# Key page scores of the first attention phase moved behind the decay sums, and the value sets of the decode step placed anew

## The reference, cut to what matters

```python
logits = jnp.einsum('nqhd,nkhd->nhqk', q, k) * (FA_HEAD_DIM ** -0.5)
decay = c_q[..., :, None] - c_k[..., None, :]          # c = cumsum(log forget values)
p = jax.nn.softmax(where(causal, logits + decay, -inf))
o = jnp.einsum('nhqk,nkhd->nqhd', p, v)
y = (o * jax.nn.silu(z)) @ w_out + b_out
x = layer_norm(alpha * x + (1 + gate) * y)
```

## Time and profile before

| | |
|---|---|
| median of 3 runs | 1765.38 us (1764.94 to 1765.78) |
| the profiled execution | 1757.93 us, span 1756.3 us, mean granted TensorE clock 0.975 |
| PE / PEld busy | 1643.2 us (94%) / 1428.1 us (81%) |
| DVE busy | 1011.8 us (58%) |
| ACT / POOL busy | 623.8 us (36%) / 420.2 us (24%) |
| DMA | 197.90 MB, mean 113 GB/s |

### The profile page before, as it was taken

The page is one execution under the profiler, slowest core; times in us unless marked ns, Lnnn a source line. Parts: engine busy times, 40 slices in busy tenths (PEclk is TensorE's granted clock), DMA queues, the critical chain, the costliest instruction groups (busy, mean ns, idle before and its releaser), DMA issues.

```text
span 1756.3 us, 27853 instructions
## 1 busy us (share of the span) xinstructions
PE 1643.2 (94%) x10080; PEld 1428.1 (81%) x10080; DVE 1011.8 (58%) x1571; ACT 623.8 (36%) x980; POOL 420.2 (24%) x414
## 2 busy tenths in 40 slices
PE   6999989999999998999887999999999999979965
PEld 4899989999999997999865777787777777757742
DVE  3433353433433437225566888879797977689436
ACT  2222122112112117224442646463636455463221
POOL 0240010110111100001221626262534344250020
PEclk8999999999999998999998999999999999999987
DMA  8481112222222221324324242424333221243474
GB/s 363 158 315 36 48 61 93 77 72 95 72 72 96 73 71 56 109 92 154 118 72 135 84 113 69 120 74 118 97 95 97 84 72 72 73 133 132 159 283 194
DMA packets 85777, 197.90 MB, mean 113 GB/s; under 512 B 16898, under 2 KB 47234, under 8 KB 83922
## 3 DMA queue, kind: packets, MB, share of 16 engines
q1 hardware_dynamic: 73154, 141.97, 24.9%
q0 software_dynamic: 12560, 55.10, 8.9%
HBM read 171.31 MB, written 34.39 MB: 117 GB/s over the span
## 4 chain that ended last, share of the span: by engine, by line
PE 77%; DVE 9%; issue 5%; DMA 3%; ACT 3%; POOL 2%; POOLq 0%; SPq 0%; DVEq 0%; ACTq 0%
PE bank L1826 20%; PE bank L1827 19%; PE bank L1828 19%; PE bank L2188 2%; PE bank L2142 2%; PE bank L2190 2%; PE bank L2189 2%; PE bank L1961 2%; PE bank L2170 1%; DVE bank L1479 1%; PE bank L2169 1%; POOL p_lo L640 1%; DMA pages<-cache_v 1%; PE bank L1941 1%; PE bank L2045 1%
## 5 line engine op out<-in xcount | busy, mean ns | idle before, releaser
L1826 PE MATMUL bank<-h_hi,w_lo 128*128 128x344 f32 x1152 | 374.5, 325 | 9.9 <-DVE h_lo L1125 8.7
L1827 PE MATMUL bank<-h_lo,w_hi 128*128 128x344 f32 x1152 | 369.0, 320 | 0.0
L1828 PE MATMUL bank<-h_hi,w_hi 128*128 128x344 f32 x1152 | 368.7, 320 | 0.0
L640 POOL TENSOR_TENSOR p_lo<-parg,p_hi 128x512 fp32r<-128x512 f32 (+1 forms) x192 | 226.8, 1199 | 161.4 <-ACT p_hi L966 160.7
L1826 PEld LDWEIGHTS bank<-h_hi,w_lo 128*128 128x128 f32 x1152 | 217.7, 189 | 14.8 <-issue 12.2
L1826 PE MATMUL bank<-x_hi,w_lo 128*128 128x512 f32 x528 | 222.1, 421 | 6.6 <-POOL x_lo L592 6.5
L1827 PEld LDWEIGHTS bank<-h_lo,w_hi 128*128 128x128 f32 x1152 | 217.8, 189 | 0.2 <-issue 0.2
L1828 PEld LDWEIGHTS bank<-h_hi,w_hi 128*128 128x128 f32 x1152 | 217.7, 189 | 0.0
L1827 PE MATMUL bank<-x_lo,w_hi 128*128 128x512 f32 x528 | 209.7, 397 | 0.0
L1828 PE MATMUL bank<-x_hi,w_hi 128*128 128x512 f32 x528 | 209.6, 397 | 0.0
L1826 PE MATMUL bank<-y_hi,w_lo 128*128 128x320 f32 (+2 forms) x512 | 177.4, 346 | 13.7 <-DVE w_lo L1083 6.5
(11 more groups left out here) (300 smaller groups left out, 2622.5 us busy)
## 6 DMA issues: line engine op xcount, KB each, us to landing
raw<-units SPq DMA_DIRECT2D x121, 512.0 KB, 3.5
scr_k<-cache_k POOLq DMA_DIRECT2D x32, 512.0 KB, 5.4
ada_ring<-w_ada SPq DMA_DIRECT2D x32, 512.0 KB, 3.3
pages<-cache_v POOLq DMA_DIRECT2D x32, 512.0 KB, 6.1
kpb<-scr_k SPq DMA_DIRECT2D x24, 512.0 KB, 4.1
ada_first<-w_ada SPq DMA_DIRECT2D x8, 1024.0 KB, 14.8
KX<-KA SPq DMA_DIRECT2D x32, 256.0 KB, 6.9
ckb<-scr_c POOLq DMA_DIRECT2D x16, 512.0 KB, 4.7
```

The lines of the kernel that those rows point to most:

```text
L640: g.tensor_tensor(p_lo[:, r, off:HALF], parg[:, r, off:HALF], p_hi[:, r, off:HALF].bitcast(F32), ALU.subtract).then_inc(S("p_ready"), 1)
L1826: mm(out, lhs_lo, rhs_hi, start=first, stop=False)
L1827: mm(out, lhs_hi, rhs_lo, start=False, stop=False)
L1828: return mm(out, lhs_hi, rhs_hi, start=False, stop=last)
```

## The change

**First phase.** On SP, the q row and the first key group of phase 0 are taken from ahead of `load_phase(0)` and issued inside it, after `KX` and raw unit (1,0), and after a wait for both rows of `ckb`. On VectorE, phase 0's four `score_mul` and `score_sum` pairs each stand one place later; the fourth is behind `kq_low(1, 0)` at the phase's end. The other phases are as before.

**Value sets.** Sets 4 and 5 go to slots 0 and 1, after sets 2 and 3; sets 6 and 7 go to slots 2 and 3, after the projection. On TensorE sets 0 and 1 are used at halves 9 and 10 (before: 11 and 12), sets 2 and 3 at halves 13 and 14 (before: between the first transposes of the end), sets 4 and 5 between the first transposes, 6 and 7 after those of block 3.

**The end.** On SP the eight `fsw` transfers also wait until all pages of sets 6 and 7 are in. `mask_o`, `gated_s` and the `fs_row` copies stand one block earlier on VectorE, `d_o`, the `fsw` matmuls, the fold and the sample's sums two blocks (the sums one) earlier on TensorE. `pages_in2` now counts sets 6 and 7.

```diff
--- before.py
+++ after.py
@@ -272,10 +272,10 @@
 
         LATE = KB - 2
         MOVED = 16 * 2 * NS * NP
-        VALUE_SLOT = (0, 1, 0, 1, 2, 3, 0, 1)
+        VALUE_SLOT = (0, 1, 0, 1, 0, 1, 2, 3)
         VALUE_IN = {0: ("pages_in0", MOVED + 16 * NP), 1: ("pages_in1", 16 * NP), 2: ("pages_in0", MOVED + 32 * NP),
-                    3: ("pages_in1", 32 * NP), 4: ("pages_in2", 32 * NP), 5: ("pages_in2", 32 * NP),
-                    6: ("pages_in0", MOVED + 48 * NP), 7: ("pages_in1", 48 * NP)}
+                    3: ("pages_in1", 32 * NP), 4: ("pages_in0", MOVED + 48 * NP), 5: ("pages_in1", 48 * NP),
+                    6: ("pages_in2", 32 * NP), 7: ("pages_in2", 32 * NP)}
         SCORED = 4 * KB
 
         KIND = (0, 1, 2, 3)
@@ -456,6 +456,12 @@
             def load_phase(j, scored):
                 load_swapped(j)
                 load_b(j + 1, 0)
+                if isinstance(j, int) and j == 0:
+                    for h in range(2):
+                        sp.wait_ge(S(f"ckb_in{h}"), 16)
+                    load_query(0)
+                    sp.wait_ge(S("pages_in0"), MOVED)
+                    load_keys(0, 0)
                 load_b(j + 1, 1)
                 load_keys(j, 1)
                 load_b(j + 1, 2)
@@ -473,9 +479,6 @@
             for q in range(4):
                 load_b(0, q)
             sp.wait_ge(S("ln1_back"), TT)
-            load_query(0)
-            sp.wait_ge(S("pages_in0"), MOVED)
-            load_keys(0, 0)
             load_phase(0, True)
             with sp.Fori(1, LATE - 1) as j:
                 load_phase(j, True)
@@ -520,6 +523,7 @@
 
             sp.wait_ge(S("r2_ready"), 2 * KB)
             sp.wait_ge(S("lo_ready"), U_FS)
+            sp.wait_ge(S("pages_in2"), 32 * NP)
             for b in range(KB):
                 sp.dma_start(fsw[:, b, :, :], units[U_FA - WB + b, :, :, :]).then_inc(S("fsw_in"), 16)
 
@@ -696,12 +700,10 @@
             for n in range(NS):
                 if n < 2:
                     pool.wait_ge(S("pages_used"), SCORED - 4 + 4 * n)
-                elif n < 4:
+                elif n < 6:
                     pool.wait_ge(S("pages_used"), SCORED + n - 1)
-                elif n == 4:
+                elif n == 6:
                     pool.wait_ge(S("fa_mm"), 2 * KB)
-                elif n >= 6:
-                    pool.wait_ge(S("pages_used"), SCORED + n - 3)
                 load_values(n)
             for name, n in (("vn_out", 16), ("k_out", 16 * KB), ("v_out", 16 * KB), ("kqv_s_out", 16)):
                 pool.wait_ge(S(name), n)
@@ -1582,6 +1584,8 @@
 
             def phase(j, more, keys):
                 later = not isinstance(j, int) or j > 0
+                late_keys = keys and not later
+                keys = keys and later
                 take_samples(j, 2)
                 kq_low(j, 1)
                 evac_s(j, 2)
@@ -1615,6 +1619,8 @@
                 z_gate(j, 0)
                 exponents(j, 2)
                 z_evac(j, 1)
+                if late_keys:
+                    score_mul(j, 0)
                 if keys:
                     score_mul(j, 1)
                 exponents(j, 3)
@@ -1623,6 +1629,8 @@
                 z_gate(j, 1)
                 if later:
                     invert(j - 1, 1, 1)
+                if late_keys:
+                    score_sum(j, 0)
                 if keys:
                     score_sum(j, 1)
                 if more:
@@ -1633,6 +1641,8 @@
                 gate_o(j, 0)
                 exponents(j, 5)
                 invert(j, 0, 0)
+                if late_keys:
+                    score_mul(j, 1)
                 if keys:
                     score_mul(j, 2)
                 exponents(j, 6)
@@ -1641,6 +1651,8 @@
                 invert(j, 0, 1)
                 exponents(j, 7)
                 divide_o(j, 0)
+                if late_keys:
+                    score_sum(j, 1)
                 if keys:
                     score_sum(j, 2)
                 if more:
@@ -1650,9 +1662,13 @@
                     evac_s(j + 1, 1)
                     split_lo(j + 1, 2)
                 exponents(j, 9)
+                if late_keys:
+                    score_mul(j, 2)
                 if keys:
                     score_mul(j, 3)
                 exponents(j, 10)
+                if late_keys:
+                    score_sum(j, 2)
                 if keys:
                     score_sum(j, 3)
                 if not more:
@@ -1661,6 +1677,9 @@
                 exponents(j, 11)
                 if more:
                     kq_low(j + 1, 0)
+                    if late_keys:
+                        score_mul(j, 3)
+                        score_sum(j, 3)
                 else:
                     lo(U_FA + 1, (U_FA + 1) % 2)
                     for k in range(2, KB - 1):
@@ -1791,29 +1810,32 @@
 
             layer_norm_stats(0, TT)
             layer_norm_stats(1, TT)
-            for t in range(2, 5):
-                finish(t - 2)
-                layer_norm_stats(t, TT)
+            finish(0)
+            layer_norm_stats(2, TT)
+            finish(1)
+            layer_norm_stats(3, TT)
+            finish(2)
+            mask_o()
+            layer_norm_stats(4, TT)
             finish(3)
-            mask_o()
+            gated_s()
             layer_norm_stats(5, TT)
             finish(4)
-            gated_s()
-            layer_norm_stats(6, TT)
-            finish(5)
             for h in range(2):
                 dve.wait_ge(S("fs_used"), h + 1)
                 v.tensor_copy(fs_row[:, h * 512:(h + 1) * 512], bank(6 + h)).then_inc(S("fs_row"), 1)
-            layer_norm_stats(7, TT)
-            finish(6)
+            layer_norm_stats(6, TT)
+            finish(5)
             dve.wait_ge(S("fs_used"), 3)
             link(v.tensor_tensor(rS[:, :, :], bank(5)[:, 0:KB * NS].rearrange("p (a b) -> p a b", b=NS),
                                  wide(col("fa_b_out"), NS), ALU.add))
             residual_s(x1S[:, :, 0:NS])
             norm_sum(rS[:, :, :], KB)
-            finish(7)
+            layer_norm_stats(7, TT)
+            finish(6)
             norm_square(3, rS[:, :, :], KB, rS[:, :, :])
             norm_var(3)
+            finish(7)
             norm_out(3, KB, "ln_g", KB, "ln_b", rS[:, :, :]).then_inc(S("ys_ready"), 1)
 
 
@@ -2366,24 +2388,28 @@
                         decode_logits()
                     if n == 8:
                         decode_weights()
-                    if n == 11:
+                    if n == 9:
                         decode_values(0)
-                    if n == 12:
+                    if n == 10:
                         decode_values(1)
+                    if n == 13:
+                        decode_values(2)
+                    if n == 14:
+                        decode_values(3)
 
             pe.wait_ge(S("r2_ready"), 2 * KB)
             ln_forward(0, r2T, TT)
             ln_forward(1, r2T, TT)
-            for n in range(2, 6):
+            for n in range(4, 6):
                 decode_values(n)
-                ln_forward(n, r2T, TT)
+                ln_forward(n - 2, r2T, TT)
             decode_values(6)
             decode_values(7)
             pe.wait_ge(S("d_step"), 4)
             for c in range(KB):
                 last = mm(bank(4)[:, c * NS:(c + 1) * NS], omask[:, c * P:(c + 1) * P], maskp[:, :], start=True, stop=True)
             last.then_inc(S("d_o"), 1)
-            ln_forward(6, r2T, TT)
+            ln_forward(4, r2T, TT)
             pe.wait_ge(S("d_step"), 5)
             pe.wait_ge(S("fsw_in"), 16 * KB)
             for h in range(2):
@@ -2391,13 +2417,15 @@
                     rows = slice(32 * (k % 4), 32 * (k % 4) + NS)
                     last = mm(bank(6 + h)[rows, :], oS[:, k, :], fsw[:, 4 * h:4 * h + 4, k, :], start=k < 4, stop=k >= 4)
                 last.then_inc(S("fs_used"), 1)
-            ln_forward(7, r2T, TT)
+            ln_forward(5, r2T, TT)
             for h in range(2):
                 pe.wait_ge(S("fs_row"), h + 1)
                 for b in range(4 * h, 4 * h + 4):
                     last = mm(bank(5)[:, b * NS:(b + 1) * NS], fs_row[:, b * P:(b + 1) * P], fold4[:, 0:NS], start=True, stop=True)
             last.then_inc(S("fs_used"), 1)
+            ln_forward(6, r2T, TT)
             sample_sum(3, 0)
+            ln_forward(7, r2T, TT)
             sample_sum(3, 1)
```

## The result

The changed kernel takes 1773.66 us (median of 6 runs, 1770.83 to 1777.14), the kernel before 1765.12 beside it (6 runs, 1758.99 to 1765.78). The ratio is 1.0064, 95% interval 1.005 to 1.0077: slower, by less than 1%. (The two medians are 8.5 us apart; the ratio, by which the runs are compared from here on, stands for 11.3 us.) The profiled execution of after has a span of 1772.3 us and took 1773.79; that of before had 1756.3. The difference of these two, 16.0 us, is more than the runs show, since the profiled execution of before is among its shortest. Whole spans don't serve for a few us: the issue of `scr_c`, ahead of which TensorE does the same work in all kernels here, falls at 922.9 us in one trace and at 928.4 in another.

What follows compares the result with a forecast made beforehand. It took TensorE to bound the kernel nearly everywhere, broken by waits for the decay sums' transfers and the last value page. -7 + 0.5 + 12.9 = +6.4 us on 1765.4 gave 1771.8 us, range 1763.5 to 1778.

Steps and rivals of the forecast that it cites:

- -6.5: First phase: net forecast in us, from -7 for the decay rows and +0.5 for the late keys.
- Decay rows, "issued by POOL at the same moment": First phase: POOL's issues stay at 931.6 and 932.1, rows land earlier, TensorE's stall falls to 3.8 us; -7 us.
- the first phase gives back everything: Rival, first phase: stall and half clock both vanish, 12.7 us, if decay rows land in 3.8 us; 1766.1; 12 in 100.
- Late keys, +0.5 (0 to 4): End of first phase: SP's row comes about 8 us later, key page (1,0) and raw (2,0) having little slack; +0.5 us.
- covered, with 1.1 us to spare: First phase's end: the fourth score pair, 2.4 us, fits VectorE's 3.5 us wait; key page 3 lands in time.
- End, +12.9: Kernel's end: pages land earlier, but `fsw` waits for them, y_out(0) for `fsw`, mask_o for y_out(0); +12.9 us.
- If the clock stays up: Final chain after y_out(0): the end's loss would be about 3 us less.
- y_out served at once: Rival, end: `fsw` does not hold up y_out(0), landing 2.6 us after issue; not slower, 1764.7; 14 in 100.
- First part does nothing: Rival, first phase: `KX` and k_out fill the engines alone, no gain there; +13.4 us, 1778.8; 12 in 100.

Runs made afterwards that it cites:

- e1: The change's first-phase edit alone (SP and VectorE) on the kernel before, value sets and end as before: 1752.84 us, ratio 0.9951.
- e2: All edits of the change but those of the first phase, against the kernel before: 1782.61 us, ratio 1.0121.
- e5: e1 with the 4 KB q-row write back ahead of the phase, its broadcast and the key page still late: 1760.29 us, ratio 0.9988.
- e3: The kernel before with only VectorE's later score products and sums in phase 0, SP's queue as before: 1763.82 us, ratio 1.0018.
- e6: e1 with raw block (1,3) issued ahead of the last key group in phase 0: 1756.27 us, ratio 0.9961 to the kernel before.
- e9: e7 with SP waiting in phase 0 for keys and raw blocks to land before the small q-row write: 1746.23 us, ratio 0.9901 to before.
- e7: Changed kernel with three y blocks ahead of `fsw` and before's end order on VectorE and TensorE, value sets still moved: 1740.48 us, ratio 0.9878 to before.
- e11: First-phase edit and three y blocks ahead of `fsw`, with value sets and end order as in the kernel before: 1748.93 us, ratio 0.9922 to before.
- e8: e7 and e6 together, raw block (1,3) ahead of the last key group in e7: 1746.04 us, ratio 0.9907 to the kernel before.
- e4: Changed kernel with y_out(0) and y_out(1) ahead of `fsw` and its page wait on SP: 1761.94 us, ratio 0.9994 to the kernel before.

## Why the prediction was right, and where its steps were not

The sign and the shape held: a gain in the first phase, a larger loss at the end, because the weights now wait for the pages, the y block for the weights, and the mask for the y block. 1771.8 was forecast, 1773.66 measured. The closeness is in part luck. The terms sum to +6.4, where the two medians give +8.5 and the ratio +11.3; the base of 1765.4 was the median of three runs, 3 us above the 1762.1 of the many runs beside the experiments, and made up for a part of it. And the two halves were wrong in opposite directions: the first phase gained more than -6.5 (-8.6 by e1), the end lost more than +12.9 (+21.3 by e2).

*Decay rows, "issued by POOL at the same moment".* This step failed. The issue hung on the landing of `scr_c`, and that on the small q-row write, which the edit takes away: 3.4 us earlier (e5 tells this from the 1.05 MB). With it the stall went, to 0.6 us and not to 3.8, and the granted clock stayed at 1.00. By the mark the gain was 11.6 us where 7 was forecast; the rival "the first phase gives back everything" (12.7) was near the truth in size, though not by the landing of 3.8 us that it asked: the rows took a median of 5.9.

The Trainium skill (DMA: Bandwidth & Descriptors, Queues, rings and completion order) says that a transfer's completion signal lands only after all earlier writes of the same DMA engine, whatever their queue. The traces agree for `scr_c`, issued behind the small write: 6.1 to 6.3 us in the four kernels that have the write there (before, e2, e3, e5), 2.2 in those that don't. The rule doesn't give the other half: raw (1,3) and, in e6, the key group are issued ahead of the write and are late too.

*Late keys, +0.5 (0 to 4).* The border gave back 2.6 us, inside the range, but "covered, with 1.1 us to spare" failed. VectorE had the time for the fourth pair, but POOL was at `p_lo` beside it and TensorE needed that: 1.0 us, in e3 and e9 as in after. The rest was SP's queue: in before SP comes to the small write 4.3 us after raw (1,3) (1003.71 and 1007.99), in after 0.6 us. So it was raw (1,3), and not the key pages or raw (2,0) that the text watched; raw (2,0) held up e1 and e9 a little later in the phase. That the write's nearness does it rests on e6 and e9; neither was faster.

*End, +12.9.* The mechanism held at each point, the size was off: +23.6 us in the traces (of it 1.3 ahead of the projection's half n = 4, in some traces with either end and not in others), +21.3 by e2. On the scale of the projection's last `fg`: pages in at 17.0 (forecast 14.9; the last lands 7.8 us after issue, not 5.3); y_out(0) issued at 20.8 (19.4) and landed at 33.1 (29.1), 12.3 us after issue and not 9.7; from there to the end 52.6 us (47.8). In the last piece the mask's and the fold's matmuls take 3.58 us each at half clock, where the sum had those of before at full clock (1.95 and 1.85 us), and VectorE waits up to 7.0 us for block 5's transposes, forecast 6. Together these make the time from the last `fg` to the span's end 8.9 us longer than forecast. "If the clock stays up" was given as a chance of 3 us less; the trace went the other way.

*y_out served at once* fell: 12.3 us. *First part does nothing* fell with e1.

What stays open: why a write of 4 KB takes 8.4 to 13.8 us here, and by what path it holds a transfer issued before it. No run changed its layout.

## What to carry to other kernels

Before a buffer-bound step is put ahead of a chain that ends the kernel, ask what its buffer waits for: here taking two calls (`mask_o` and `gated_s`) out from behind `finish(2)` was worth 14 us, and taking the first two stores out from behind the weights 12. Each is measured with the other left as it was; they act on the same wait, so they don't simply add. In this kernel, value work moved into a busy stage paid only where the transfers at its end were issued in the order in which they were needed: the same sets lost 21 us with the stores and the mask in the wrong place (e2), and gained 8 with both put right (e7 against e11). Work moved into another engine's idle time is not free when a third engine works beside it: look at what runs there. And when an issue time is carried over as unchanged, follow its releaser back one more step.

## Hardware behaviour that was not expected

A 4 KB write that the program lays out in 4-byte pieces, on SP's queue, took 10.7 us before (919.21 to 929.96) and 10.9 after (1005.54 to 1016.44), from its issue to that of the transfer that waits for it; over all phases and traces it was 8.4 to 13.8. Beside it the write of the decay sums from POOL's queue took 6.1 us instead of 2.2, and the 512 KB transfer issued 0.5 to 0.6 us ahead of it 8.0 to 11.1 us where it is the raw block (nine traces) and 7.8 and 8.6 where it is the key group (e8, e6); raw blocks have a median of 3.5, key groups of 4.1. Issued 4.3 to 5.0 us behind the raw block, as in before, e2 and e9, it let that land in 4.7 to 4.9.

A VectorE product of 128x1024 numbers slowed POOL's `p_lo` beside it: the pair took 2.40 to 2.45 us in the eight traces where the product starts 34.7 to 34.9 us after the second `mb`, and 1.41 or 1.42 in the six where it starts later (35.1 and on) or stands elsewhere. In after, e4 and e11, POOL's `w_sc` starts while VectorE is at `QA`, and the two `QA` take 4.0 to 4.1 us; in the others 2.47.
